# Expert stages of a two-layer kernel: token rows picked by one-hot products, expert results stored in slot order and fetched per token at the end, blocks placed evenly

## The reference, cut to what matters

```
expert_id = g_sel[:, None] * MOE_EXPERTS_PER_GROUP + top_idx        # two experts for each token
...
def expert_block(args):
    xb, e = args
    return (jax.nn.silu(xb @ w_gate[e]) * (xb @ w_up[e])) @ w_down[e]
...
return jax.ops.segment_sum(yp[dest] * w_s[:, None].astype(h.dtype), tok_s, num_segments=T)
```

## Time and profile before

| | |
|---|---|
| median of 3 runs | 2247.38 us (2246.84 to 2250.01) |
| profiled execution, its own time | 2246.04 us |
| its span in the trace | 2244.2 us |
| TensorE / VectorE / ScalarE / GpSimd busy | 86% / 43% / 30% / 4% of the span |
| mean DMA rate over the span | 275 GB/s |
| rounds of layer 0, first product to last | 1066.5 to 1554 us |
| rounds of layer 1, first product to last | 1730.6 to 2219 us |

### The profile page before, as it was taken

How to read it: one execution, slowest core, us unless ns; L and a number is a source line. 1 busy time by engine, 2 the same in 40 slices (tenths; PEclk the granted TensorE clock), 3 DMA queues, 4 the chain that set the end, 5 groups by cost and what they waited for, 6 DMA issues and landing times.

```text
span 2244.2 us, 29502 instructions
## 1 busy us (share of the span) xinstructions
PE 1929.4 (86%) x9453; PEld 1085.2 (48%) x9454; DVE 956.4 (43%) x2077; ACT 665.8 (30%) x1053; POOL 100.0 (4%) x133
## 2 busy tenths in 40 slices
PE   8878999999999999997976887777897967877885
PEld 4534777745577775554432433333764423323332
DVE  2273888312478534444432432334224423323333
ACT  1142000012400002132543543444102534434443
POOL 2000000000000000000000000000000000000000
PEclk9869999999899999998998998999997988888998
DMA  8502898433179543305899999996645999999994
GB/s 282 201 6 99 325 343 312 178 141 143 66 277 358 197 167 132 124 31 207 334 421 383 360 412 407 407 416 260 258 160 221 385 421 379 415 421 389 411 394 166
DMA packets 84611, 617.69 MB, mean 275 GB/s; under 512 B 16289, under 2 KB 16609, under 8 KB 21809
## 3 DMA queue, kind: packets, MB, share of 16 engines
q1 hardware_dynamic: 68912, 544.70, 61.3%
q0 software_dynamic: 14752, 69.77, 8.3%
q10 hardware_dynamic: 864, 2.19, 0.2%
HBM read 621.84 MB, written 19.92 MB: 286 GB/s over the span
## 4 chain that ended last, share of the span: by engine, by line
PE 67%; DMA 19%; DVE 5%; issue 3%; ACT 3%; DVEq 2%; SPq 1%; ACTq 0%; POOLq 0%
PE ps L843 25%; PE ps L1216 15%; PE ps L1053 14%; DMA big<-in_w_up 7%; PE ps L1065 7%; DMA big<-in_w_down 5%; DMA big<-in_w_gate 5%; PE ps L1218 3%; PE ps L857 2%; ACT big L1684 2%; DVEq L2413 1%; DVE hT L2421 1%; PE ps L1245 1%; DMA c_res<-f_rows,big 1%; PE ps L1208 1%
## 5 line engine op out<-in xcount | busy, mean ns | idle before, releaser
L1216 PE MATMUL ps<-big,hT 128*32 128x512 f32 x3072 | 723.5, 627 | 144.0 <-ACT big L1684 140.5
L1218 PE MATMUL ps<-big,hT 128*32 x1536 | 722.3, 627 | 0.0
L1684 ACT COPY big<-big 128x1024 f32 x384 | 395.0, 1046 | 526.2 <-PE ps L1218 267.1
L2400 DVE TENSOR_SCALAR big<-big 128x1024 f32 x384 | 263.0, 696 | 623.0 <-PE ps L1218 375.6
L1216 PEld LDWEIGHTS ps<-big,hT 128*32 128x32 f32 x3072 | 200.5, 114 | 541.3 <-DVE big L2400 276.0
L1053 PE MATMUL ps<-hT,big 128*128 128x256 f32 x1408 | 311.1, 379 | 0.0
L843 PE MATMUL ps<-big,hT 128*128 128x512 f32 (+4 forms) x792 | 299.7, 537 | 4.8 <-DMA big<-in_dense 2.5
L1053 PEld LDWEIGHTS ps<-hT,big 128*128 128x128 f32 x1408 | 266.7, 190 | 49.0 <-issue 14.8
L843 PEld LDWEIGHTS ps<-big,hT 128*128 128x128 f32 x792 | 144.4, 195 | 149.3 <-issue 139.7
L843 PE MATMUL ps<-big 64*30 64x256 f32 (+14 forms) x704 | 161.4, 512 | 30.7 <-DVE big L2350 8.3
L1218 PEld LDWEIGHTS ps<-big,hT 128*32 128x32 f32 x1536 | 164.8, 114 | 6.1 <-issue 0.9
(11 more groups left out here) (333 smaller groups left out, 1176.2 us busy)
## 6 DMA issues: line engine op xcount, KB each, us to landing
big<-in_w_down SPq DMA_DIRECT2D x128, 1024.0 KB
big<-in_w_gate SPq DMA_DIRECT2D x128, 1024.0 KB, 12.1
big<-in_w_up SPq DMA_DIRECT2D x128, 1024.0 KB, 12.9
big<-in_dense SPq DMA_DIRECT2D x52, 1536.0 KB, 8.3
big<-in_dense POOLq DMA_DIRECT2D x28, 2048.0 KB, 9.9
big<-in_dense SPq DMA_DIRECT2D x21, 2048.0 KB, 8.3
big<-in_dense SPq DMA_DIRECT2D x5, 1024.0 KB, 7.5
big<-y_rows SPq DMA_DIRECT2D x4, 1024.0 KB, 6.2
```

Of the source, the lines that this page charges most:

```text
L1216: nc.tensor.matmul(ps[g * SLOTS:(g + 1) * SLOTS, bank, :], xT[:, k, g * SLOTS:(g + 1) * SLOTS], side[:, g - 1, quarter % 2, at:at + BW], s ...
L1218: return nc.tensor.matmul(ps[0:SLOTS, bank, :], xT[:, k, 0:SLOTS], experts3[:, bass.ds(here, 1), kind * CH + row:kind * CH + row + BW] .re ...
L1684: nc.scalar.copy(side[:, 1, quarter % 2, :], experts3[:, bass.ds(there, 1), lo:lo + QW] .rearrange("p a n -> p (a n)")).then_inc(s["side2_ ...
L2400: ts(side[:, 0, quarter % 2, :], experts3[:, bass.ds(there, 1), lo:lo + QW].rearrange("p a n -> p (a n)"), 1.0, None, mult).then_inc(s["si ...
```

## The change

**Rows in.** `f_rows` and the gathers go. VectorE makes two comparisons for each half of the tokens (`first_pick`, `second_pick`) between the slot numbers 0 to 95 and `rel`, the token's slot less 96 times the round; the sum is a 128x96 matrix of zeros and ones, and TensorE multiplies `fN` by it, which picks and transposes in one step (`rows_T`: 8 pieces x 2 halves of the tokens). In the first round this needs only `rel`, not the table.

**Rows out.** Each round's 96 results go to `y_rows` in slot order by a plain DMA on ScalarE's queue (`store`), all 96 rows of 15 rounds. Token weights are applied later, not in `hm`. In the last round GpSimd fetches each token's two rows by four indirect DMAs (`fetch`), and VectorE adds them with their weights. The last round's results are not stored: `turn_last` and `hot` make the transposed, weighted one-hot matrix, and TensorE spreads the 96 rows over the tokens with four products. The store's last 96 rows are zeros, written once during the first FFN.

**Placement.** The first block of an expert is its number of earlier blocks plus the smaller of the spare blocks and the running maximum of 3e/2 less the earlier blocks: no expert begins before block 3e/2 while spare blocks last, two experts to a round.

**Other.** SyncE no longer waits for the store and the fetch, so the convolution's weights stand right behind the experts'. Layer 1's gate rows are made by TensorE behind the first three steps of the convolution, which now has 6 PSUM banks instead of 8. `f_rows`' writes go.

```diff
-        f_rows = nc.dram_tensor("f_rows", [S, D], fp32, kind="Internal").ap()
-        y_rows = nc.dram_tensor("y_rows", [2 * S, D], fp32, kind="Internal").ap()
+        y_rows = [nc.dram_tensor(f"y_rows{l}", [ROUNDS * ROWS, D], fp32, kind="Internal").ap() for l in range(DEPTH)]
...
@@ TensorE, rows_T @@
-                        pe.wait_ge(s["rows_gathered"].sem, s["rows_gathered"].at(b * 16 + 16))
+                        pe.wait_ge(s["pick_ready"].sem, s["pick_ready"].at(b * TC + TC))
...
-                        rows = xe[0:ROWS, :].rearrange("t (p k) -> t k p", k=KT)[:, 4 * h + k, :]
-                        ins = nc.tensor.transpose(ps[:, h, k * ROWS:(k + 1) * ROWS], rows, const["ident"][0:ROWS, 0:ROWS])
+                        for t in range(T):
+                            ins = nc.tensor.matmul(ps[:, h, k * ROWS:(k + 1) * ROWS], fN_by_k[t][:, 4 * h + k, :],
+                                                   onehot[:, t, :], start=t == 0, stop=t == T - 1)
...
@@ TensorE, end of the rounds @@
+                pe.wait_ge(m["hot_ready"].sem, m["hot_ready"].end)
+                for c in range(T):
+                    for h in range(2):
+                        if c == 0:
+                            pe.wait_ge(m["last_ready"].sem, m["last_ready"].at(h + 1))
+                        mm(ps[:, 2 * c + h, :], hot[0:ROWS, c, :], ym[0:ROWS, h * BW:(h + 1) * BW], True, True,
+                           m["last_spread"].sem)
...
@@ TensorE, convolution @@
+                if t < 3:
+                    if t:
+                        g = st["g1_1"]["gate_copied"]
+                        pe.wait_ge(g.sem, g.at(2 * t))
+                    row_pair("g1_1", t, CONV_BANKS)
...
@@ ScalarE @@
+                def store(b):
+                    act.wait_ge(s["y_ready"].sem, s["y_ready"].at(b + 1))
+                    act.dma_start(rows[b * ROWS:(b + 1) * ROWS, :], ym[0:ROWS, :]).then_inc(s["y_stored"].sem, 16)
...
@@ VectorE, route @@
-                L(ts(rest[:, 0:E], ps[:, 3, E:2 * E], -1.0, float(NB), mult, add))
-                L(tt(pad_i[:, 0:E], rest[:, 0:E], rt[:, 1, :], mult))
-                L(ts(pad_i[:, 0:E], pad_i[:, 0:E], E.bit_length() - 1, None, ALU.logical_shift_right))
-                L(tt(pst, ps[:, 3, 0:E], pad_i[:, 0:E], add))
+                ts(rest, ps[:, 3, E:E + 1], -1.0, float(NB), mult, add)
+                L(tt(lead[:, 0, first:], rt[:, 1, :], ps[:, 3, 0:E], sub))
+                for i, n in enumerate(SHIFTS):
+                    old, new = lead[:, i % 2, :], lead[:, 1 - i % 2, :]
+                    L(tt(new[:, first:], old[:, first:], old[:, first - n:first - n + E], ALU.max))
+                L(stt(pst, lead[:, len(SHIFTS) % 2, first:], rest, ps[:, 3, 0:E], ALU.min, add))
...
+            def first_pick(s, b):
+                for t in range(TC):
+                    ts(onehot[:, t, :], const["iota"][:, 0:ROWS], rel[:, t, bass.ds(b, 1)], None, ALU.is_equal)\
+                        .then_inc(s["pick_step"].sem, 1)
...
@@ VectorE, end of the rounds @@
+                for c in range(T):
+                    v.wait_ge(m[f"y_fetched_{c}"].sem, m[f"y_fetched_{c}"].end)
+                    for k in range(2):
+                        link(v, stt(lat(c), y01[c][:, k, :], tok_w[:, k * T + c:k * T + c + 1], lat(c), mult, add))
+                v.wait_ge(done.sem, done.end)
+                v.wait_ge(s["y_stored"].sem, s["y_stored"].end)
+                for h in range(2):
+                    cols = slice(h * BW, (h + 1) * BW)
+                    tt(ym[0:ROWS, cols], ps[0:ROWS, 5 + h, :], gb2[0:ROWS, 0, cols], mult).then_inc(m["last_ready"].sem, 1)
+                for i, (out, c, h) in enumerate(parts):
+                    v.wait_ge(m["last_spread"].sem, m["last_spread"].at(i + 1))
+                    tt(out, out, ps[:, 2 * c + h, :], add).then_inc(m["combined"].sem, 1)
...
@@ GpSimd, fetch @@
+                pool.wait_ge(s["y_stored"].sem, s["y_stored"].end)
+                pool.wait_ge(s["xT_ready"].sem, s["xT_ready"].end)
+                for c in range(TC):
+                    if c:
+                        pool.wait_ge(s["quarter_done"].sem, s["quarter_done"].at(12 * (ROUNDS - 1) + 4))
+                    for k in range(2):
+                        q = k * TC + c
+                        nc.gpsimd.indirect_dma_start(
+                            out=y01[c][:, k, :], out_offset=None, in_=y_rows[layer][:, :],
+                            in_offset=bass.IndirectOffsetOnAxis(ap=row_i[:, q:q + 1], axis=0),
+                            bounds_check=ROUNDS * ROWS - 1, oob_is_err=False).then_inc(m[f"y_fetched_{c}"].sem, 16)
```

More of the change, by code:

```diff
@@ L1691, in experts @@
                 for b in range(ROUNDS):
-                    for j in range(2, 6):
+                    for j in range(2, 4):
+                        copy(b, there, j)
+                    if b:
+                        store(b - 1)
+                    for j in range(4, 6):
                         copy(b, there, j)
@@ L2798, in _ @@
             aux("ffn0", [(convw, dram["convw"][0])])
+            s = st["zero"]
+            pool.wait_ge(s["zeros_ready"].sem, s["zeros_ready"].end)
+            for l in range(DEPTH):
+                pool.dma_start(y_rows[l][(ROUNDS - 1) * ROWS:ROUNDS * ROWS, :], zeros[0:ROWS, :])\
+                    .then_inc(s["rows_zeroed"].sem, 16)
+            pool.wait_ge(s["rows_zeroed"].sem, s["rows_zeroed"].end)
             mod_loads(0, "normF0")
```

275 lines of the change are left out of this document (129 added, 146 removed).

## The result

| | before | after |
|---|---|---|
| median of all runs, us | 2247.11 | 2274.8 |
| span of the profiled execution, us | 2244.2 | 2273.8 |
| mean granted clock of TensorE in it | 0.93 | 0.93 |

The ratio is 1.0127, 95% interval 1.0109 to 1.0144: slower by 1.3%, where 2198 us, 2.2% faster, was forecast. Without one storage order, which the first experiment changes, the same change measures 0.9772.

What follows compares the result with a forecast made beforehand. Rounds were taken to wait for expert weights, the loader now and then for a round, with serial stretches around them. 2246.0 - 11.2 - 30 - 13.0 + 5.2 = 2197.0, as a median 2198 us; range 2184 to 2212 with 60%.

Steps and rivals of the forecast that it cites:

- TensorE's round: Expert rounds: TensorE's work, 24.5 us plus picks less transposes and a wait, was put at 27.7, faster than transfers.
- 32 x 0.15 = 4.8 us: Expert rounds: 32 picking instructions at 0.15 us each, against 1.3 us for the eight transposes they replace.
- a term at nothing: Items counted as 0 us: VectorE's four pick comparisons a round, ScalarE's store issue, and zeros written in the first FFN.
- the sign of TensorE: Profile sign that would show the forecast wrong through TensorE: rounds of 33 us with DMA below 400 GB/s.
- no row has that form: Remark that no profile row shows a strided 128-row operand, whose slow loading could bring a pick to 0.25 us.
- The third rival: TensorE becomes the bound, slower than before, 4%; its point is a 30.8 us round, picks at 0.25 us each.
- First product: Routing to each layer's first expert product: shorter table work and picks bring it 5.6 us earlier, twice; bounds -3 and -8.
- Rounds: First to last expert product: -12 us in layer 0, -18 in layer 1; bounds for both together -10 and -50.
- the threes: Rounds needing three new experts under the old placement, where long waits stand; round 4 began 16 us late.
- the hole at layer 0's round 7: After the change, a 69-token expert fills round 6 alone and round 7 needs three: a loading hole of about 5 us.
- The end of the rounds: Last expert product to last add: faster adds and four spreading products save 6.7 us in layer 0, 6.3 in layer 1.
- Gate rows: Six products, 12 instructions at 0.43 us, moved between the convolution's products with nothing covering them: +5.2 us.

Runs made afterwards that it cites:

- contig_picks: The first experiment: changed kernel with normed rows stored so a pick's 128 operand columns lie side by side instead of 8 words apart; 2195.49 us, ratio 0.9772.
- store_twice: As contig_picks, but every round's 96 result rows are stored a second time, to an array nobody reads; 2222.85 us.
- even_before: The kernel before the change with only the even placement of the experts' blocks added; 2254.42 us, ratio 1.0039.
- contig_double: As contig_picks, but every block of picking products is made twice, 64 instructions a round; 2223.85 us, ratio 0.9892.
- half_picks: Changed kernel with picking products for the first 128 tokens only, 16 strided instructions a round instead of 32; 2192.69 us, ratio 0.9765.
- gather_96: As even_before, but every round's gather and scatter are issued for 96 rows instead of 128; 2252.38 us.

## Why the prediction was wrong

What failed is TensorE's round, which the working put at 27.7 us, below the transfers' 30.8. The first step is the size of one term: "32 x 0.15 = 4.8 us". The picks took 8.1. The second is a term at nothing, without a word on it: the clock. In after it is at its half level from the middle of the picks until 3 us behind them, and that costs the round 1.5 us more. So 31.7 to 33.4 us came out, above the transfers, and with it what the prediction gave as the sign of TensorE: rounds of 33 us with DMA below 400.

The working took the price from 16 instructions with 128 rows and 36 columns, and gave 0.25 as the upper bound; the bound was right and the choice wrong. The row chosen has none of the operand's spacing, and "no row has that form" closed the search too soon. What was missed is the rule of the Trainium skill on lines of 16 bytes, on the page that the prediction cites for something else ("SBUF — State Buffer").

The price alone would hardly have turned the sign. In the prediction's own sum 0.25 us an instruction gives a round of 30.9, level with the transfers. Contiguous picks made to last 7.5 us give 2223.9, 1.1% faster than before; the half microsecond a round by which they are shorter than the strided ones is 17 us at most, an estimate from 32 rounds. The rest of the way to 2274.8 came with the clock, which the strided picks take to its half level and the contiguous ones of the same length don't. The third rival, TensorE as the bound, was the right mechanism with 4%, and it named the strided operand. Its point, 0.25 us an instruction, was met, by the price and the clock together.

That contig_picks comes out at 2195.5, near the 2198 that was forecast for the change, is in part luck: several terms were off, in both directions. The other steps, read in contig_picks, where TensorE isn't the bound:
- First product, counted from routing's last transposes: -4.6 in layer 0 and -7.1 in layer 1, for -5.6 in each. In after -2.0 and -4.8, since 32 picks took 7.95 us there. In layer 0 even the contiguous picks cost 0.21 each and not 0.15, at the half level of the clock.
- Rounds: -15.2 and -17.2 for -12 and -18; the interval forecast, 30.8, is 30.7, and TensorE's round 26.2 to 26.8 for 27.7. The direct stores were counted rightly (store_twice). Gathers and scatters were not: I gave them 10 us a layer by their bytes, and a round under transfers is 2.5 us longer with them, 40 if every round waits on transfers. So, read between even_before and contig_picks, the change takes 1.6 us off such a round instead of adding 4 us to a layer, and the holes before were smaller than I made them.
- Placement: the threes and the hole at layer 0's round 7 (35.5 to 35.8 us, forecast 5 us long) are as described, and undoing the placement gives back 26 to 30 us. That it loses 7 alone was not foreseen.
- The end of the rounds: -7.0 and -5.9 for -6.7 and -6.3; in layer 0 TensorE is idle 4.2 us, then takes 5.4 (after) or 6.4 (contig_picks) for the four products, forecast 5.3; nothing waits for the fetches.
- Gate rows: three pairs of 1.72 us between products, as forecast.
- The convolution's weights don't start 20 us earlier: the load issues with the last product in after (1576.7), and 6 us behind it before (1560.3). Nothing waited for them, as said.

## What to carry to other kernels

When a product takes its stationary operand out of rows that are stored another way, look at the bytes between neighbouring columns: at 8 they load at full speed, at 16 and 32 the whole 128x128 fp32 picking instruction took twice its time at the full clock. The rearranged write ahead of 16 rounds of reads cost little: VectorE's two instructions took 2.07 and 2.03 us instead of 1.28 and 1.23, in a stretch in which it waited for TensorE anyway. A price taken from a near row must share the operand that is in doubt. And an engine that is just under the bound isn't free: a queue's head start is worth something only while the engine behind it is faster.

## What the runs showed of the hardware

- The weight load of 128x128 fp32 words has a step in its price: by the pages 335 ns mean at 8 words (after), 329 at 4, 220 at 2, 217 at 1 (contig_picks) and 195 in contig_double, where the clock was at its full level in nearly all rounds.
- The price of the strided pick doesn't go with TensorE's clock and that of the contiguous one does: 4.03 and 4.05 us for 16 strided ones at 0.50 and 1.00 (after), and for contiguous ones 0.21 us each at 0.51 and 0.125 at 1.00 (contig_picks).
- TensorE's clock can fall to its half level while the engine is hardly ever idle: 0.89 over a round with 30.95 busy us of 31.8, at 0.50 from the second half of the strided picks on; 1.00 with 28.76 of 29.7 and contiguous ones (contig_double), and 1.00 in an early round with half as many strided ones (half_picks).
- An indirect transfer counts a row that is out of bounds whole in the memory's traffic and moves nothing for it: 128 rows issued instead of 96 are 4.19 MB more read and 4.19 MB more written over 64 transfers, and 2048 more packets of under 512 bytes, with the same bytes in packets (even_before, gather_96). The time is the same. The 16.8 MB more that is read before than after (621.84 and 605.06 MB) is 32 x 128 x 4 KB.
- The busy share of the DMA engines doesn't tell whether transfers hold a kernel: a round of after has 1.00 at 397 GB/s with TensorE as the bound, where full is 1.01 at 422.
